# The first norm of an encoder layer computed with features on partitions, without turning the input on TensorE

## The reference

```python
h = rms_norm(x, norm_mix)                  # x * rsqrt(mean(x*x) + eps) * w
x = x + hybrid_mixer(h, ...)               # proj = h @ w_in; a Fourier branch and a gated recurrence; @ w_out
h = rms_norm(x, norm_ffn)
x = x + expert_choice_ffn(h, ...)          # 16 experts, each takes 2 * n_tok / 16 tokens
y = rms_norm(x, norm_final)
```

## Time and profile before

| | us |
|---|---|
| median of 3 runs | 2578.57 |
| lowest, highest | 2577.72, 2580.89 |
| the profiled execution: its time | 2578.97 |
| its span in the profile | 2577.2 |
| PE busy | 2521.5 (98%) |
| DVE busy | 1648.9 (64%) |
| ACT busy | 1366.5 (53%) |
| POOL busy | 267.9 (10%) |

### The profile page before, as it was taken

One profiled execution on the slowest core, in us unless ns is written; L12 is line 12 of the kernel. 1 busy time (PEld: TensorE's weight loads), 2 busy tenths in 40 slices (PEclk: granted clock), 3 DMA queues, 4 the chain that ended last, 5 costly groups with the idle time before them and its releaser, 6 DMA issues.

```text
span 2577.2 us, 45337 instructions
## 1 busy us (share of the span) xinstructions
PE 2521.5 (98%) x18610; PEld 2280.4 (88%) x18610; DVE 1648.9 (64%) x1927; ACT 1366.5 (53%) x1559; POOL 267.9 (10%) x238
## 2 busy tenths in 40 slices
PE   8999999999997999999999999999999999999998
PEld 6777777887877999999999999999999999999997
DVE  6555555435387766767666676766767667676767
ACT  6434353424445555555556555555555556555556
POOL 3102020101101010010101101010010101101020
PEclk9999999999997999999999999999999999999999
DMA  4101010135327676676767667676676767667677
GB/s 158 33 15 55 2 55 2 61 129 209 132 99 299 225 256 235 247 251 230 250 227 254 239 237 256 224 257 234 247 251 231 250 227 254 239 236 257 223 259 276
DMA packets 62486, 503.73 MB, mean 195 GB/s; under 512 B 7568, under 2 KB 8080, under 8 KB 37808
## 3 DMA queue, kind: packets, MB, share of 16 engines
q1 hardware_dynamic: 46224, 448.88, 47.9%
q0 software_dynamic: 16160, 53.38, 7.0%
HBM read 465.07 MB, written 37.22 MB: 195 GB/s over the span
## 4 chain that ended last, share of the span: by engine, by line
PE 67%; DVE 1%; ACT 1%; DMA 0%; issue 0%; POOL 0%; POOLq 0%; DVEq 0%; ACTq 0%
PE up_banks_b L1990 15%; PE up_banks_a L1990 15%; PE up_banks_a L1993 6%; PE up_banks_b L1993 6%; PE up_banks_b L2010 2%; PE up_banks_b L2008 2%; PE up_banks_b L2009 2%; PE up_banks_b L2007 2%; PE up_banks_a L2011 2%; PE up_banks_b L2011 2%; PE up_banks_a L2010 2%; PE up_banks_a L2008 2%; PE up_banks_a L2007 2%; PE up_banks_a L2009 2%; PE up_banks_b L1988 1%; PE up_banks_a L1988 1%
## 5 line engine op out<-in xcount | busy, mean ns | idle before, releaser
L1813 DVE TENSOR_TENSOR big_lo<-ew_raw,big_hi 128x4096 fp32r<-128x4096 f32 x192 | 849.6, 4425 | 419.5 <-ACT big_hi L1653 419.4
L1653 ACT CAST big_hi<-ew_raw 128x4096 fp32r<-128x4096 f32 x192 | 697.2, 3631 | 507.1 <-PE up_banks_a L1990 224.3
L1990 PE MATMUL up_banks_b<-x_parts,big_hi 128*128 128x384 f32 x2048 | 582.9, 356 | 0.0
L1990 PE MATMUL up_banks_a<-x_parts,big_hi 128*128 128x384 f32 x2016 | 573.8, 356 | 0.0
L1993 PE MATMUL up_banks_b<-x_parts,big_lo 128*128 128x192 f32 x1792 | 449.0, 251 | 0.0
L1993 PE MATMUL up_banks_a<-x_parts,big_lo 128*128 128x192 f32 x1764 | 442.0, 251 | 0.0
L1990 PEld LDWEIGHTS up_banks_b<-x_parts,big_hi 128*128 128x128 f32 x2048 | 371.0, 189 | 0.0
L1990 PEld LDWEIGHTS up_banks_a<-x_parts,big_hi 128*128 128x128 f32 x2016 | 365.1, 189 | 0.6
L1993 PEld LDWEIGHTS up_banks_b<-x_parts,big_lo 128*128 128x128 f32 x1792 | 341.4, 191 | 0.0
L1993 PEld LDWEIGHTS up_banks_a<-x_parts,big_lo 128*128 128x128 f32 x1764 | 336.1, 191 | 0.6
L64 PE MATMUL bank<-big_hi,w_hi 128*128 128x512 f32 x576 | 236.8, 411 | 0.0
(11 more groups left out here) (308 smaller groups left out, 4078.4 us busy)
## 6 DMA issues: line engine op xcount, KB each, us to landing
ew_raw<-in_expert_weights SPq DMA_DIRECT2D x192, 2048.0 KB, 7.8
w_raw<-in_w_heads SPq DMA_DIRECT2D x48, 256.0 KB, 2.7
x_in<-in_x SPq DMA_DIRECT2D x12, 512.0 KB, 4.1
x_d<-in_x POOLq DMA_DIRECT2D x12, 512.0 KB, 4.2
residual<-x_d POOLq DMA_DIRECT2D x12, 512.0 KB, 2.9
ffn_in<-h_and_xT_d POOLq DMA_DIRECT2D x12, 512.0 KB, 2.9
ew_raw<-residual SPq DMA_DIRECT2D x12, 512.0 KB, 6.4
tab<-in_tables POOLq DMA_DIRECT2D x10, 512.0 KB, 7.7
```

The source lines that it names most:

```text
L1653: nc.scalar.copy(w_hi[:, c % RING], raw[:, c % RAW]).then_inc(hi_done, 1)
L1813: nc.vector.tensor_tensor(w_lo[:, c % RING], raw[:, c % RAW], w_hi[:, c % RING].bitcast(F32), ALU.subtract).then_inc(lo_done, 1)
L1990: last = nc.tensor.matmul(out[:, 0:2 * CAP], hi, x[:, k], start=n == 0, stop=n == KT - 1, skip_group_check=True)
```

## The change

The input comes a second time, laid out by the host as `x_cols` [128, 8, 1536]: features on partitions. The 12 turns, the identity for them, the gain spread over all partitions (512 KB) and the tile loop are gone. The norm now works on three blocks b of 512 tokens in 8 slices k. For each block:

- SP loads 8 pieces of 128 x 512 (256 KB each).
- ACT squares each slice; DVE adds them up (7 additions, two square buffers between them).
- One PE product of a broadcast column of ones with the sum puts each token's total on all 128 partitions, in a PSUM bank (`total`, 128 x 512).
- ACT takes the root of all 128 x 512 in place (`root`), DVE the reciprocal of all 128 x 512 in place (`invert`).
- DVE scales slice by slice (`normalize`, 128 x 512), ACT casts to the high part (`high`), and DVE or POOL subtracts (`low`): DVE for block 0 and for slices 4 to 7 of block 1, POOL for slices 0 to 3 of block 1 and for block 2, all behind its ten first weight pieces.

PE makes the products of V and G of block 0 together, slice by slice as the low parts come, then Q, with V's turn after Q's third slice. The totals of block 1 come on PE behind Q, those of block 2 behind ZB. Pieces 1 and 2 of the weights change places. The squares of the blocks, the casts of the weights, the Exp and the first gates have new places, written out by hand; the last slices of block 2 are scaled during the first levels of block 0. The buffers of the norm are no longer its own but later ones of the phase (`kq`, `decay`, `gate`, `k_tok`, `keys`, `o_acc`).

```diff
@@ class HeadWeights
+    def place(self, m):
+        m = {1: 2, 2: 1}.get(m, m)
+        return m // (2 * NJ), m // 2 % NJ, slice((m % 2) * (KT // 2), (m % 2 + 1) * (KT // 2))
...
@@ class InputNorm
+    def load(self, sp, b, p):
+        if b:
+            sp.wait_ge(self.x_loaded[p], 32 * b)
+        for k in (2 * p, 2 * p + 1):
+            sp.dma_start(self.x[b][k], self.x_cols[:, k, self.cols(b)]).then_inc(self.x_loaded[p], 16)
...
+    def square(self, act, b, k):
+        n = KT * b + k
+        act.wait_ge(self.x_loaded[k // 2], 32 * (b + 1))
+        if n >= 2:
+            act.wait_ge(self.added, self.adds(n - 2))
+        self.nc.scalar.activation(self.squares[n % 2], self.x[b][k], ACT.Square).then_inc(self.squared, 1)
...
+    def total(self, pe, b):
+        pe.wait_ge(self.added, (KT - 1) * (b + 1))
+        self.nc.tensor.matmul(self.totals[b], self.ones[:].to_broadcast([P, P]), self.added_up, start=True, stop=True)\
+            .then_inc(self.totalled, 1)
+    def root(self, act, b):
+        act.wait_ge(self.totalled, b + 1)
+        self.nc.scalar.activation(self.totals[b], self.totals[b], ACT.Sqrt, scale=1.0 / D, bias=self.eps[:])\
             .then_inc(self.rooted, 1)
+    def invert(self, dve, b):
+        dve.wait_ge(self.rooted, b + 1)
+        self.nc.vector.reciprocal(self.totals[b], self.totals[b]).then_inc(self.inverted, 1)
+        dve.wait_ge(self.inverted, b + 1)
+    def normalize(self, dve, b, k):
+        dve.wait_ge(self.squared, KT * b + k + 2)
+        self.nc.vector.scalar_tensor_tensor(out=self.x[b][k], in0=self.x[b][k], scalar=self.nm[:, k:k + 1],
+                                            in1=self.totals[b], op0=ALU.mult, op1=ALU.mult).then_inc(self.h_ready, 1)
+    def high(self, act, b, k):
+        act.wait_ge(self.h_ready, KT * b + k + 1)
+        self.nc.scalar.copy(self.hT_hi[:, k, self.cols(b)], self.x[b][k]).then_inc(self.hi_done, 1)
+    def low(self, eng, on, b, k, done):
+        eng.wait_ge(self.hi_done, KT * b + k + 1)
+        on.tensor_tensor(self.hT_lo[:, k, self.cols(b)], self.x[b][k], self.hT_hi[:, k, self.cols(b)].bitcast(F32),
+                         ALU.subtract).then_inc(done, 1)
...
@@ block.gpsimd
                 for m in range(W_HALVES):
+                    if m == FIRST_HEAD:
+                        for b, ks in ((1, range(LATE_FROM)), (2, range(KT))):
+                            for k in ks:
+                                norm.low(pool, nc.gpsimd, b, k, norm.late_lo_done)
                     weights.low(pool, m)
@@ block.scalar
+                squares(0, 0, 1, 2, 3)
+                weights.high(act, 0)
+                squares(0, 4, 5)
+                weights.high(act, 1)
+                squares(0, 6, 7)
+                norm.root(act, 0)
+                for k in range(KT):
+                    norm.high(act, 0, k)
+                    if k in (1, 3, 5, 6):
+                        weights.high(act, {1: 2, 3: 3, 5: 4, 6: 5}[k])
+                    if k in (2, 3):
+                        squares(1, k - 2)
+                squares(1, 2, 3, 4)
+                take_projection(("proj", 0, V))
+                squares(1, 5, 6, 7)
+                weights.high(act, 6)
+                take_values(("vt", 0))
+                norm.root(act, 1)
+                norm.high(act, 1, 0)
+                norm.high(act, 1, 1)
+                act.wait_ge(dve_step, 1)
+                nc.scalar.activation(lbw[:, 1], lbw[:, 0], ACT.Exp).then_inc(lb_exp, 1)
+                take_projection(("proj", 0, G))
+                for k in range(2, KT):
+                    norm.high(act, 1, k)
+                    if k in (3, 4, 5):
+                        weights.high(act, k + 4)
+                    if k == 4:
+                        take_projection(("proj", 0, Q))
+                squares(2, 0, 1)
                 for ev in timeline:
...
+                    if ev == ("proj", 0, ZF):
+                        squares(2, 2, 3, 4, 5, 6, 7)
                     if kind == "proj":
...
+                        if ev == ("proj", 0, ZB):
+                            norm.root(act, 2)
+                            for k in range(LATE_FROM):
+                                norm.high(act, 2, k)
@@ block.vector
+                add_squares(0)
...
+                norm.invert(dve, 0)
+                norm.normalize(dve, 0, 0)
+                for k in range(KT):
+                    if k + 1 < KT:
+                        norm.normalize(dve, 0, k + 1)
+                    norm.low(dve, nc.vector, 0, k, norm.lo_done)
+                add_squares(1)
+                norm.invert(dve, 1)
+                for k in range(KT):
+                    norm.normalize(dve, 1, k)
+                    if k == 4:
+                        take_gate(("gates", 0, V))
+                        take_gate(("gates", 0, G))
+                for k in range(LATE_FROM, KT):
+                    norm.low(dve, nc.vector, 1, k, norm.lo_done)
+                take_gate(("gates", 0, Q))
+                add_squares(2)
...
+                        if ev == ("gates", 0, ZB):
+                            norm.invert(dve, 2)
+                            for k in range(LATE_FROM):
+                                norm.normalize(dve, 2, k)
@@ block.tensor
+                pe.wait_ge(const_set, 2)
+                norm.total(pe, 0)
+                for k in range(KT):
+                    pe.wait_ge(norm.lo_done, k + 1)
+                    product(V, k)
+                    product(G, k)
+                for k in range(KT):
+                    product(Q, k)
+                    if k == 2:
+                        turn_values(("vt", 0))
+                norm.total(pe, 1)
                 for ev in timeline:
...
                         for k in range(KT // 2) if kind == "begin" else range(KT // 2, KT):
+                            if n == 1 and j == V and k >= LATE_FROM:
+                                pe.wait_ge(norm.lo_done, KT + k - LATE_FROM + 1)
+                            elif 1 <= n < NB and j == V:
+                                pe.wait_ge(norm.late_lo_done, LATE_FROM * (n - 1) + k + 1)
...
+                        if ev == ("proj", 0, ZB):
+                            norm.total(pe, 2)
```

More of the change, by code:

```diff
@@ new lines, in hold, with cols, warm @@
+    def hold(self, x, squares, added_up, totals, ones, eps):
+        self.x, self.squares, self.added_up, self.totals, self.ones, self.eps = x, squares, added_up, totals, ones, eps
+    def cols(self, b):
+        return slice(b * BLK, (b + 1) * BLK)
+    def load(self, sp, b, p):
[3 more added lines that the diff above has]
+            sp.dma_start(self.x[b][k], self.x_cols[:, k, self.cols(b)]).then_inc(self.x_loaded[p], 16)
+    def warm(self, act, out):
+        self.nc.scalar.activation(out, self.eps[:], ACT.Sqrt).then_inc(self.squared, 1)
@@ L300, in heads_phase @@
         eps = sb("eps_b", [P, 1])
+        norm = InputNorm(nc, sb, sem, x_cols, weights, hT_hi, hT_lo)
         o_acc = [pb(f"o_acc{b}", [P, CH, P]) for b in range(NB)]
@@ L461, in _ @@
                 sp.dma_start(lb[:], lb_params).then_inc(const_loaded, 16)
+                norm.load(sp, 1, 0)
+                norm.load(sp, 1, 1)
+                for i in range(2):
+                    weights.load(sp, 2 + i)
+                    norm.load(sp, 1, 2 + i)
+                for i in range(4):
+                    weights.load(sp, 4 + i)
+                    norm.load(sp, 2, i)
+                for m in range(8, FIRST_HEAD):
+                    weights.load(sp, m)
                 stores = iter([("bc",) + ev[1:] for ev in timeline if ev[0] == "out"])
@@ new lines, in squares @@
+                def squares(b, *ks):
+                    for k in ks:
+                        norm.square(act, b, k)
+                act.wait_ge(const_set, 1)
+                norm.warm(act, rms[:, 0, 0:1])
+                squares(0, 0, 1, 2, 3)
[10 more added lines that the diff above has]
+                        squares(1, k - 2)
@@ L772, in _ @@
             def _(pe):
-                early = [(j, k) for j in EARLY for k in range(KT)]
-                def products(count):
-                    for j, k in early[:count]:
-                        i, m = fill_of[("proj", 0, j)]
-                        if k == 0 and m:
-                            pe.wait_ge(bank_read[i], m)
-                        if k % (KT // 2) == 0:
-                            pe.wait_ge(weights.lo_done, 2 * j + k // (KT // 2) + 1)
-                        last = three_products(nc, bank[i][:].rearrange("p c t -> p (c t)"), w_hi[:, j, k], w_lo[:, j, k],
-                                              hT_hi[:, k, 0:BLK], hT_lo[:, k, 0:BLK], k == 0, k == KT - 1)
-                        if k == KT - 1:
-                            last.then_inc(bank_filled[i], 1)
-                    del early[:count]
@@ L788, in after_turns, with product @@
-                def after_turns(t):
-                    if t == EARLY_AT:
```

(25 more changed lines are left out.)

287 lines of the change are left out of this document (115 added, 172 removed).

## The result

The changed kernel takes 2600.97 us (median of 4, 2598.05 to 2603.43) against 2578.45 (median of 4 in the same comparison): ratio 1.0086, 95% interval 1.0073 to 1.0098, so 22.5 us slower. The forecast was slower, 2590.1, with a range to 2595: the direction was right, the size half of what came, and outside of the range. The profiled execution took 2601.6, its span is 22.6 above that of before.

A forecast was written before the change was run, and what follows sets the result against it. PE, at work in 98% of the span, was taken as the bound, so a later turn of V of block 1 (77.0 instead of 65.46) shifts the end: 2578.97 + 11.5 = 2590.5, as a median 2590.1, range 2582 to 2595.

The forecast's parts named there:

- PE idle ahead of ZF: PE stands idle from 38.9 to 52.6 us, between the total of block 1 and ZF: 13.7 us.
- turn of V of block 1: PE's turn right ahead of the first level: 77.0 instead of 65.46, 11.5 us later, shifting the end equally.
- the wait for piece 7 with its releaser: ZF on PE waits for weight piece 7, cast late by ACT, until POOL's low part ends at 52.5.
- the line on DVE that sets the turn: DVE's casts, low parts, additions, gates, reciprocal and scalings ahead of ACT's V copy put block 1's V turn at 77.0.
- no difference after it but a constant: Sign of a right forecast: behind the turn of V of block 1, both kernels differ by a constant shift only.
- On DVE 0.69 for two inputs: Rate for DVE instructions with two inputs: 0.69 us each, the next beginning about 0.08 earlier than it ends.
- DVE delivers a slice every 1.3 us: In V and G of block 0, DVE delivers a slice every 1.3 us, PE needs 1.4, so DVE hides.
- The last pair is there at 9.8: At the start, block 0's last slices land at 9.8 us: 0.8 MB in the first 5 us, then 380 GB/s.
- 1.3 us for each start: Charge for PE's slow pace, 0.43 instead of 0.23 us a product, after each long idle time: 1.3 us.
- 0.3 for the copy that frees its bank: Ahead of Q on PE: 0.3 us waiting for the copy that frees its bank.
- Nothing, or at most 0.15 in each slot: Added DVE and ACT work in the first levels hides: nothing, or at most 0.15 us per slot of the first kind.
- B: Rival, slower still, 2592.5 to 2596: reciprocal 4.3, total 1.7, pieces under 380 GB/s, a level slot that slips; 18%.

The follow-up runs named there:

- e4_pool: Changed kernel with POOL's later subtractions, for the ten first weight pieces and blocks 1 and 2, cut to 8 columns (output not the reference's): 2594.49 us, ratio 1.0062.
- e8_order: Changed kernel with all eight x slices of block 0 loaded ahead of weight pieces 0 and 1, these cast behind the squares: 2600.12 us.
- e5_busy: Changed kernel with unread products in PE's idle time: 15 behind block 0's totals, 52 behind block 1's, 12 ahead of block 1's V turn: 2603.02 us, ratio 1.0088.
- e12_busy10: Changed kernel with 10 unread products on PE, only ahead of the turn of V of block 1: 2600.28 us.
- e1_pieces: Changed kernel with ACT casting weight piece 7 right behind piece 6, pieces 8 and 9 behind block 1's root: 2595.26 us, ratio 1.0063.
- e3_recip: Changed kernel with the three reciprocals on 8 of 512 columns (output not the reference's): 2592.24 us, ratio 1.0058.
- the tables: Changed kernel with Exp and G's sigmoid, with both table loads, moved into ACT's wait behind block 1's root: 2598.53 us, ratio 1.0077.
- e10_psum: Changed kernel with narrow root and reciprocal, reordered casts and totals, x loaded first, 12 scaled slices in PSUM: 2581.16 us, ratio 1.0001 to the kernel before.

## Why the prediction was wrong in size

By its own steps, forecast and measured:

| step | forecast | measured |
|---|---|---|
| last addition of block 0 ends | 11.7 | 14.7 |
| reciprocal of 128 x 512 | 3.7 | 3.36 |
| first product | 19.6 | 23.31 |
| V, G, Q: first product to the totals of block 1 | 18.6 | 20.9 |
| PE idle ahead of ZF | 13.7 | 12.6 |
| ZF and ZB | 12.2 | 13.4 |
| wait for additions of block 2 | 0 | 1.8 |
| turn of V of block 1 | 77.0 | 85.48 |
| turn to next turn, against 32.85 before | +0 | +2.4 |
| in all | +11.5 | +22.5 |

The mechanisms were right: the wait for piece 7 with its releaser, the reciprocal, the line on DVE that sets the turn. Of the signs that I named, the reciprocal (3.36), the idle time ahead of ZF, its releaser and the wait ahead of the turn (3.1) came; the first product (not at 19 to 20.5), the turn (not at 75 to 79) and "no difference after it but a constant" did not. The idle time came out close, but both of its ends were 5 to 6 us late. One mechanism was missing: that POOL's subtractions stop DVE's. The other terms were mis-sized.

- **"On DVE 0.69 for two inputs"** is the step that failed most. That row is of a DVE instruction whose 11 instances all took 691 to 694 ns. With POOL subtracting it is up to 1.8, and the change gives POOL 12 more low parts and DVE 21 additions and 12 low parts with both inputs in SBUF. `e4_pool` is worth 6.5 us by the medians and 6.6 at the turn. "DVE delivers a slice every 1.3 us" was 1.7 (eight in 13.7 us, 21.13 to 34.85), so DVE did not hide behind PE, and the additions of block 2 took 7.4 us (65.61 to 72.98) where I had 5.0, and made PE wait where I had no wait. The trace of the kernel before had the effect. By line, L722 has a mean of 732 ns in the heads phase, but a median of 685 and a maximum of 1808 over 71 instances; one of the long ones, and a TENSOR_SCALAR that otherwise takes 0.48, stand beside POOL's work:

```profile
129.17 3.00 POOL L96 TENSOR_TENSOR w_lo<-w_raw,w_hi 128x512 fp32r<-128x512 f32 x2 [2.18 <-ACT w_hi L92]
...
129.21 1.81 DVE L722 TENSOR_TENSOR kq<-kq,decay 128x512 f32<-128x512 f32 x1
130.94 1.52 DVE L695 TENSOR_SCALAR kq<-sig,one_less_lb 128x512 f32<-128x512 f32 x1
```

- **The start.** "The last pair is there at 9.8": its square began at 11.86. The rate of the earlier trace rows was carried over from pieces of 512 KB, and I let the weight pieces cost only their bytes. Between 6 and 10 us the DMAs moved 314 and 363 GB/s, in the kernel before 412 and 416 (two stretches of 2 us each); whether the size of the pieces made that difference, no run tests. Two of the 3.0 us are this and the order of the loads, the rest the additions beside POOL; `e8_order` takes 2.2 of it back. The totals took 2.05 instead of 1.0: the trace has two MATMULs for that one product.
- **The pace after idle time.** I took 1.3 us for each start, from one start of 2.3 us behind half-busy turns. Products stood 0.43 apart from 23.31 to 28.5 and from 57.84 to 62.6, which is 2.4 and 2.2 us more than at the upper level. In the first two places DVE's line covered it (`e5_busy`). The third is behind the turn: I had PE waiting 3.5 us there and still charged no start. It cost 1.5 (`e12_busy10`).
- **"0.3 for the copy that frees its bank"**, ahead of Q: PE waited 1.3, since ACT's copy of V (37.54) stands behind three squares of block 1, which wait for DVE's additions. That is 1.0 of the 2.3 between 18.6 and 20.9; the rest is DVE's pace in V and G.
- **"Nothing, or at most 0.15 in each slot"** for the levels: two slots were 3.69 instead of 3.33, by POOL's subtractions (`e4_pool`), and the first was 4.90 for the reason above; 2.4 together.

The range was too narrow because its upper end added the unknowns of one kind, instruction widths, and none for engines in each other's way. Of the rivals B came nearest. Three of its reasons came (the total, the pieces at less than 380 GB/s, a slot of the levels), its reciprocal of 4.3 did not (3.36), and the largest part, POOL against DVE, is in none of the rivals.

The price of the wait that I had called the main one was checked, too: it is 5.7 us (`e1_pieces`), since behind it DVE's line is nearly as long. The reciprocals are 8.7 (`e3_recip`), POOL against DVE 6.5 with POOL's own 1.0 in it (`e4_pool`), the tables 2.4; all are medians against 2600.97, they overlap and may not be added up. Taken together with a better order they come to the 20 us between the changed kernel and `e10_psum`.

## What to carry to other kernels

A statistic that is one column when tokens lie on partitions becomes a full-width one when features do: count root, reciprocal and broadcast at the new width before counting the turns that are saved, and narrow them again. When a wait on the critical engine is 12 us long, look for the line on the other engines that ends just behind it: taking away the wait alone gave 5.7. Give every place where an engine is expected to wait long its slow restart, also the last one. And price DVE instructions by rows in which POOL does what it will do in the new place; where a line's mean lies above its median, look at its longest instances and at what ran beside them.

## What was not expected of the hardware

- A DVE subtraction of 128 x 512 with both inputs in SBUF takes 0.68 alone and 1.1 to 1.8 us when it begins beside a POOL subtraction of 128 x 512 (1.28 to 1.8); the one read from PSUM and SBUF takes 0.68 to 0.69 in both cases (12 of 12 in `e10_psum`). It stands still rather than runs slower: in the changed kernel those of 23.83, 28.72, 30.42, 33.37 and 57.83 us, of 1.12 to 1.78 us, all end 0.54 to 0.55 behind the end of POOL's instruction. The other way round POOL waits: its row at 27.53, begun 0.07 behind a DVE subtraction, took 1.76. A POOL memset, which reads nothing, did not do it: beside it two DVE additions took 0.69 each (`e4_pool`, 12.26 and 13.06). A DVE TENSOR_SCALAR of 128 x 512, with one such input, was held as well: 1.52 for 0.48 (130.94 in the kernel before). The Trainium skill's page "GPSIMD Engine Reference", in "Specifications", says that POOL shares its SBUF interfaces with VectorE, and that VectorE instructions with two SBUF inputs contend; these runs agree, and give the price. The same rule would have pointed at this case's largest missing term, had I weighed it.
- The reciprocal on DVE takes 164, 171, 203 to 213 and 3364 ns for 1, 4, 8 and 512 columns: 6.25 ns a column beyond 8. By the clock of 0.96 GHz in the Trainium skill's page "VectorE: DVE Perf Modes" ("Specifications") that is six cycles a column; the eight cycles that I had tried on the page's repeat count of 8 don't come out.
- A product of plain f32 with 512 columns shows as two MATMULs in the trace, 2.05 us together at the slow pace (14.88) and 1.0 to 1.1 otherwise (44.24, 73.03).
